# A diffusion trunk step with routed experts: column halves of each weight slot in the rounds of 64 expert slots, and a fourth column group of the large rounds that starts one step later

## What is computed

```
def moe_ffn(h, router, w_gu, w_down):
    logits = (h @ router).astype(jnp.float32)
    top_v, top_i = lax.top_k(logits, TOP_K)
    w = jax.nn.softmax(top_v, axis=-1)
    combine = jnp.sum(jax.nn.one_hot(top_i, N_EXPERTS, dtype=jnp.float32) * w[..., None], axis=-2)
    gu = jnp.einsum('btd,edf->btef', h, w_gu)
    g, u = jnp.split(gu, 2, axis=-1)
    act = jax.nn.silu(g) * u * combine[..., None].astype(h.dtype)
    return jnp.einsum('btef,efd->btd', act, w_down)
```

## Time and profile before

| | |
|---|---|
| median of 3 runs | 2507.28 us (2504.83 to 2510.34) |
| the profiled execution: its time, its span | 2505.68 us, 2503.8 us |
| TensorE (PE) busy | 2269.1 us, 91% of the span |
| PE's share of the chain that ended last | 85% |
| DMA moved | 552.11 MB, mean 221 GB/s |
| rounds 0 to 6 on PE, with the start of the wide round, in the two expert layers | 811.86 us to about 1156, 2071.54 us to about 2415 |

### The profile page before, as it was taken

The page is one execution under the profiler, slowest core; times in us unless marked ns, Lnnn a source line. Parts: engine busy times, 40 slices in busy tenths (PEclk is TensorE's granted clock), DMA queues, the critical chain, the costliest instruction groups (busy, mean ns, idle before and its releaser), DMA issues.

```text
span 2503.8 us, 44069 instructions
## 1 busy us (share of the span) xinstructions
PE 2269.1 (91%) x19591; PEld 1626.1 (65%) x19591; DVE 473.9 (19%) x1344; ACT 394.2 (16%) x829; POOL 67.2 (3%) x111
## 2 busy tenths in 40 slices
PE   5998998999998998899799589999988989989897
PEld 3875667888887544445475478888868875434354
DVE  1323432000113200000202320002334432000001
ACT  1122223000101000000202320001133320000000
POOL 5000000000000000000100000000000000000000
PEclk8999999999998999999899589999999989999998
DMA  9759787653354899997677176513430067999981
GB/s 321 217 197 391 281 314 202 199 151 101 113 194 139 291 380 338 385 331 275 184 237 292 37 209 194 151 34 118 151 101 7 11 219 254 384 337 381 334 322 42
DMA packets 356158, 552.11 MB, mean 221 GB/s; under 512 B 11392, under 2 KB 311168, under 8 KB 343472
## 3 DMA queue, kind: packets, MB, share of 16 engines
q1 hardware_dynamic: 344208, 525.31, 60.7%
q0 software_dynamic: 5840, 18.11, 2.8%
q10 hardware_dynamic: 5920, 5.78, 0.7%
HBM read 537.64 MB, written 15.98 MB: 221 GB/s over the span
## 4 chain that ended last, share of the span: by engine, by line
PE 85%; DVE 5%; DMA 3%; ACT 3%; issue 3%; ACTq 0%; POOL 0%; SPq 0%; DVEq 0%; POOLq 0%
PE ps L632 83%; DMA ring<-in_ada_w 2%; ACT ring L1362 2%; ACT work L1362 1%; PE ps L1002 0%; DVE ring L1908 0%; DMA work<-y_rows,work 0%; DVE work L1771 0%; DMA y_rows<-work 0%; DVE ring L1913 0%; DVE ring L1898 0%; DVE ring L2043 0%; ACT hT L1362 0%; PE ps L1099 0%; DVE ring L1890 0%
## 5 line engine op out<-in xcount | busy, mean ns | idle before, releaser
L632 PE MATMUL ps<-ring,work 128*32 128x384 f32 (+6 forms) x7752 | 710.4, 453 | 69.1 <-issue 37.4
L632 PE MATMUL ps<-hT,ring 128*128 128x256 f32 x3200 | 704.9, 380 | 3.2 <-ACT hT L1362 2.1
L632 PEld LDWEIGHTS ps<-hT,ring 128*128 128x128 f32 x3200 | 607.0, 190 | 98.2 <-ACT work L1362 6.9
L632 PEld LDWEIGHTS ps<-ring,work 128*32 128x32 f32 (+2 forms) x7752 | 339.6, 116 | 415.0 <-issue 292.0
L1362 ACT ACTIVATE work<-ps 128x256 f32<-128x256 f32 (+5 forms) x252 | 108.7, 444 | 1433.5 <-PE ps L632 1266.9
L632 PE MATMUL ps<-work,ring 128*128 128x256 f32 (+1 forms) x1344 | 290.9, 376 | 10.8 <-DVE work L1975 6.2
L632 PEld LDWEIGHTS ps<-work,ring 128*128 128x128 f32 (+1 forms) x1344 | 243.9, 189 | 48.3 <-DVE work L1975 8.6
L632 PE MATMUL ps<-ring 64*64 64x64 f32 (+1 forms) x4192 | 185.3, 230 | 17.6 <-ACT ring L1362 7.2
L632 PEld LDWEIGHTS ps<-ring 64*64 64x64 f32 x4192 | 162.6, 139 | 57.0 <-ACT ring L1362 24.2
L1362 ACT ACTIVATE ring<-ps 128x512 f32<-128x512 f32 (+3 forms) x224 | 106.9, 483 | 351.7 <-PE ps L632 315.3
L632 PE MATMUL ps<-ring,csil 128*2 128x512 f32 x768 | 98.2, 601 | 22.7 <-DMA ring<-in_ada_w 22.7
(11 more groups left out here) (253 smaller groups left out, 966.6 us busy)
## 6 DMA issues: line engine op xcount, KB each, us to landing
ring<-in_moe_w_gu SPq DMA_DIRECT2D x96, 1536.0 KB, 13.7
ring<-in_ada_w SPq DMA_DIRECT2D x96, 1024.0 KB, 7.6
ring<-in_moe_w_down SPq DMA_DIRECT2D x48, 1536.0 KB, 16.0
ring<-in_ff_w_gu SPq DMA_DIRECT2D x88, 512.0 KB, 5.8
ring<-in_dn_w_in SPq DMA_DIRECT2D x32, 1024.0 KB, 5.5
ring<-in_moe_w_gu SPq DMA_DIRECT2D x32, 1024.0 KB, 8.5
ring<-in_ff_w_down SPq DMA_DIRECT2D x44, 512.0 KB, 6.8
ring<-in_moe_w_down SPq DMA_DIRECT2D x32, 512.0 KB, 10.1
```

The lines of the kernel that those rows point to most:

```text
L632: return pe.matmul(out, lhsT, rhs, start=start, stop=stop, **kw)
```

## The change

- `columns` and `gate_up` (large): step 0 leaves the fourth column group idle. In steps 1 and 2 that group does two matmuls, 256 and 128 columns wide (`D_PARTS`), so that its 3 x 256 columns are done in two steps. The wait for slots 2 and 3 moves to step 1. Of silu, product, transposes and copy, steps 1 and 2 cover all 128 partitions; silu and the product are now one operation each instead of two. `down(3)` finds the last two blocks of its input by `D_AT`.
- Small rounds go through the same three steps as the large ones. `halves` gives two column groups one half of a slot and the other two groups the other half: 192 columns for a slot of 384, and in step 1 also 128 for a `_D` slot. `p_gu` counts up after each slot, and after each of the two `_D` slots in step 1.
- There are three turns in a small round instead of two, and each is built of pieces of 64 rows (`turn_small`), with four or five copies on ScalarE (`turned_small`) where there was one.
- SP no longer waits for `p_dn` before it loads slots 2 and 3.

The core of the diff:

```
                         for j in (0, 1, 4, 5, 2, 3, 6, 7, 8, 9, 10):
                             if j in GU_FREE:
                                 sp.wait_ge(moe["p_gu"], (done[0] + r) * 6 + GU_FREE[j])
-                                if j in (GATE_D, UP_D):
-                                    sp.wait_ge(moe["p_dn"], (done[0] + r) * 4 + 1)
...
                 def columns(q, s, j, j_d, bank):
                     landed(q, j)
-                    if s == 0:
+                    if s == 1:
                         landed(q, j_d)
...
                     for k in range(KC):
                         for b in range(STEPS):
-                            mm(ps[BLK * b:BLK * (b + 1), bank, 0:GW], xg[:, k, BLK * b:BLK * (b + 1)], w[:, k, :],
-                               k == 0, k == KC - 1)
-                        ins = mm(ps[CAP:P, bank, 0:DW], xg[:, k, BLK * s:BLK * (s + 1)], w_d[:, k, :],
-                                 k == 0, k == KC - 1)
+                            ins = mm(ps[BLK * b:BLK * (b + 1), bank, 0:GW], xg[:, k, BLK * b:BLK * (b + 1)], w[:, k, :],
+                                     k == 0, k == KC - 1)
+                        for n, (b, at, c, width) in enumerate(D_PARTS.get(s, ())):
+                            ins = mm(ps[CAP:P, bank, at:at + width], xg[:, k, BLK * b:BLK * (b + 1)],
+                                     w_d[:, k, c:c + width], k == 0 and n == 0, k == KC - 1, skip_group_check=True)
...
+                def halves(q, j, width, bank, at):
+                    landed(q, j)
+                    w = weights(j, 2 * width)
                     for k in range(KC):
+                        for x in range(2):
                             for b in range(2):
                                 t = 2 * x + b
+                                ins = mm(ps[BLK * t:BLK * (t + 1), bank, at:at + width], xg[:, k, BLK * b:BLK * (b + 1)],
+                                         w[:, k, x * width:(x + 1) * width], k == 0 and at == 0, k == KC - 1,
+                                         skip_group_check=True)
+                    return ins
...
+                    for j, j_d, bank in ((GATE[s], GATE_D, PG[s]), (UP[s], UP_D, PU[s])):
+                        ins = halves(q, j, HW, bank, 0)
+                        if s == 1:
+                            ins = halves(q, j_d, P, bank, HW)
+                        ins.then_inc(moe["p_gu"], 1)
...
                 def turn_small(q, s):
+                    pe.wait_ge(moe["d_act"], q * 3 + (s + 1))
...
+                    lo, hi = slice(0, 64), slice(64, P)
+                    pe.transpose(ps[:, 6, 0:P], ma_s[:, s, 0:P], ident)
                     if s == 1:
+                        pe.transpose(ps[:, 6, HW:HW + P], ma_s[:, s, HW:HW + P], ident)
+                    pe.transpose(ps[lo, 6, 64:P], ma_s[lo, s, P:HW], ident[lo, lo])
+                    pe.transpose(ps[:, 7, 0:64], ma_s[hi, s, 64:HW], ident[hi, hi])
+                    ins = mm(ps[hi, 7, 64:P], ma_s[hi, s, 0:64], ident[hi, hi])
+                    ins.then_inc(moe["p_tr"], 1)
...
                 def small(q):
...
+                    gate_up_small(q, 0)
+                    gate_up_small(q, 1)
                     turn_small(q, 0)
                     down_small(q, 0)
+                    gate_up_small(q, 2)
+                    turn_small(q, 1)
+                    down_small(q, 1)
                     pe.wait_ge(moe["d_g"], q + (i + 2))
                     gather(0)
                     gather(1)
+                    turn_small(q, 2)
+                    down_small(q, 2)
+                    down_small(q, 3)
...
+                def turned_small(q, s):
+                    act.wait_ge(moe["p_tr"], q * 3 + (s + 1))
+                    act.wait_ge(moe["p_dn"], q * 4)
+                    lo, hi = slice(0, 64), slice(64, P)
+                    f(ma_T[:, s, 0:64], ps[:, 6, 0:64], ACT.Copy)
+                    f(ma_T[lo, s, 64:P], ps[lo, 6, 64:P], ACT.Copy)
+                    if s == 1:
+                        f(ma_T[:, s, HW:HW + P], ps[:, 6, HW:HW + P], ACT.Copy)
+                    f(ma_T[:, s, P:HW], ps[:, 7, 0:64], ACT.Copy)
+                    f(ma_T[hi, s, 64:P], ps[hi, 7, 64:P], ACT.Copy).then_inc(moe["a_at"], 1)
```

More of the change, by code:

```diff
@@ L1097, in turn @@
                         pe.wait_ge(moe["a_at"], q * 3 + s)
-                    for c in range(2):
-                        pe.transpose(ps[:, 6, c * P:(c + 1) * P], ma_s[:, s, c * P:(c + 1) * P], ident)
-                    pe.transpose(ps[:, 6, 2 * P:2 * P + CAP], ma_s[0:CAP, s, 2 * P:3 * P], ident[0:CAP, 0:CAP]) \
-                        .then_inc(moe["p_tr"], 1)
+                    rows = P if s else CAP
+                    for c in range(3):
+                        ins = pe.transpose(ps[:, 6, c * P:c * P + rows], ma_s[0:rows, s, c * P:(c + 1) * P],
+                                           ident[0:rows, 0:rows])
+                    ins.then_inc(moe["p_tr"], 1)
                 def down(q, s, first):
@@ L1113, in down @@
                         for b in range(STEPS):
[L1114 to L1115 removed]
+                            of, at = (s, P * (c % 3) + BLK * b) if s < 3 else (D_AT[c, b][0], P * D_AT[c, b][1] + CAP)
+                            lhsT = ma_T[:, of, at:at + BLK]
                             for g in range(4):
@@ L1128, in columns_small @@
                                 t = 2 * x + b
-                                ins = mm(ps[BLK * t:BLK * (t + 1), bank, 0:width], xg[:, k, BLK * b:BLK * (b + 1)],
-                                         weights(j, width)[:, k, :], k == 0, k == KC - 1)
-                    ins.then_inc(moe["p_gu"], done)
-                def turn_small(q, s):
-                    pe.wait_ge(moe["d_act"], q * 3 + (1 + 2 * s))
-                    if s == 1:
-                        pe.wait_ge(moe["a_at"], q * 3 + 1)
-                    for c in range(2 if s else 3):
-                        ins = pe.transpose(ps[:, 6, c * P:(c + 1) * P], ma_s[:, s, c * P:(c + 1) * P], ident)
-                    if s == 1:
-                        ins = pe.transpose(ps[:, 6, 2 * P:2 * P + 64], ma_s[0:64, s, 2 * P:3 * P], ident[0:64, 0:64])
-                    ins.then_inc(moe["p_tr"], 1 + s)
+                                ins = mm(ps[BLK * t:BLK * (t + 1), bank, at:at + width], xg[:, k, BLK * b:BLK * (b + 1)],
+                                         w[:, k, x * width:(x + 1) * width], k == 0 and at == 0, k == KC - 1,
+                                         skip_group_check=True)
@@ L1566, in gated @@
                         act.wait_ge(moe["d_act"], q * 3 + s)
-                    f(mg_s[0:CAP, DW:GW], ps[0:CAP, PG[s], DW:GW], ACT.Silu)
-                    f(mg_s[:, 0:DW], ps[:, PG[s], 0:DW], ACT.Silu).then_inc(moe["a_silu"], 1)
+                    rows = P if s else CAP
+                    f(mg_s[0:rows, :], ps[0:rows, PG[s], 0:GW], ACT.Silu).then_inc(moe["a_silu"], 1)
                 def turned(q, s, first):
@@ L1573, in turned @@
                         act.wait_ge(moe["p_dn"], q * 4)
-                    f(ma_T[:, s, 0:2 * P + CAP], ps[:, 6, 0:2 * P + CAP], ACT.Copy).then_inc(moe["a_at"], 1)
+                    if s == 0:
+                        f(ma_T[:, s, :].rearrange("p (c n) -> p c n", c=3)[:, :, 0:CAP], ps4(6)[:, 0:3, 0:CAP], ACT.Copy) \
+                            .then_inc(moe["a_at"], 1)
+                    else:
+                        f(ma_T[:, s, :], ps[:, 6, 0:GW], ACT.Copy).then_inc(moe["a_at"], 1)
                 def output(q):
@@ L1600, in store_small, with gated_small @@
                             .then_inc(moe["y_out"], 16)
+                def gated_small(q, s):
+                    act.wait_ge(moe["p_gu"], q * 6 + (2 * s + 1))
+                    act.wait_ge(moe["d_act"], q * 3 + s)
+                    f(mg_s[:, 0:SW[s]], ps[:, PG[s], 0:SW[s]], ACT.Silu).then_inc(moe["a_silu"], 1)
+                def turned_small(q, s):
[8 more added lines that the diff above has]
+                    f(ma_T[hi, s, 64:P], ps[hi, 7, 64:P], ACT.Copy).then_inc(moe["a_at"], 1)
                 def small(r):
@@ L1604, in small @@
                     output(q - 1)
[L1605 to L1607 removed]
+                    gated_small(q, 0)
                     store(q - 1, r - 1)
[L1609 to L1615 removed]
+                    gated_small(q, 1)
+                    turned_small(q, 0)
+                    gated_small(q, 2)
+                    turned_small(q, 1)
                     tokens(q + 1)
[L1617 to L1618 removed]
+                    turned_small(q, 2)
                 def body(r, first):
@@ L2224, in gated @@
                         dve.wait_ge(moe["p_tr"], q * 3 + (s - 2))
-                    tt(ma_s[0:CAP, s, DW:GW], mg_s[0:CAP, DW:GW], ps[0:CAP, PU[s], DW:GW], ALU.mult)
-                    tt(ma_s[:, s, 0:DW], mg_s[:, 0:DW], ps[:, PU[s], 0:DW], ALU.mult).then_inc(moe["d_act"], 1)
+                    rows = P if s else CAP
```

(6 more changed lines are left out.)

73 lines of the change are left out of this document (26 added, 47 removed).

## The result

| | before | after |
|---|---|---|
| median, 8 runs each | 2507.78 us (2504.78 to 2510.34) | 2518.69 us (2516.34 to 2526.11) |
| ratio, 95% interval | | 1.005 (1.0037 to 1.0064) |
| the profiled execution: time, span | 2505.68, 2503.8 us | 2518.7, 2516.9 us |

The change makes the kernel slower by 0.5%. I had said 2509, range 2496 to 2523, with 0.35 for slower. Of the ten executions of a later run (e8) one took 3050.63 us at a mean granted clock of 0.739 of full speed and is left out of that run's ratio.

What follows compares the result with a forecast made beforehand. TensorE (PE), busy 91% of the span, was taken as the bound, with instruction fetch stalling it at loop tops. Terms +7.8 + 0.8 + 2.4 - 8.2 = +2.8 us on 2505.68 gave 2508.5, stated as 2509, range 2496 to 2523.

Steps and rivals of the forecast that it cites:

- columns, turns, one join more: Small rounds: narrower columns save 1.5 us, three turns and one more join cost 2.8; +1.3 each, +7.8 us for six.
- large rounds: Large rounds: five matmuls stand where four did, 0.1 us a round, +0.8 us for eight.
- slots 2 and 3 due later, SP: Weight loads: slots 2 and 3 needed 10.3 us later and SP's wait dropped; 0, since PE waits for no weight.
- code blocks between jumps: Small rounds, steps 0 and 1: three instruction blocks used in 4.6 us each, fetched in 5.2; 0.4 each, +2.4 us.
- the four tops: Loop tops, two per layer: moved within their code blocks, shortening the second wait, 3.5 each layer 1, 0.6 layer 3; -8.2 us.
- rival 1: Small rounds: code cannot keep up at 6 us per block, each losing 2.6 us; +13, 2522 us, chance 0.22.
- Rival 2: Small-round turns: shape changes and copies at their upper bound; +12, 2520 us, chance 0.13.
- high bound: Small-round turns: 0.3 us for each shape change and no overlap of copies; +4.8 us a round instead of +2.8.
- Rival 3: Turns and loop tops: cheap turns, and a jump losing its second wait in both layers; 2497 us, chance 0.18.
- Rival 4: Loop tops: weights cost PE after all, releasing slots singly gives back up to 7 us each; 2480 us, chance 0.07.
- the last step: Final sum: profiled 2505.68 us plus 2.8 gives 2508.5; median before 1.6 above that execution; forecast stated as 2509.

Runs made afterwards that it cites:

- e8: The changed kernel with each small-round turn as three 128x128 transposes and one copy of 384 columns, as before the change: 2503.30 us, ratio 0.9986.
- e4: The changed kernel with TensorE's loop over rounds 1 to 6 written out, other engines keeping theirs: 2480.47 us, ratio 0.99.
- e7: The changed kernel loading only part of each weight slot from round 1 on, so DMA is lightly loaded: 2484.04 us, one execution.
- e11: The kernel before, loading only part of each weight slot from round 1 on, as in e7: 2484.82 us, one execution.
- e2: The kernel before with only the large rounds of the change, all small rounds as before: 2482.30 us, ratio 0.9913.
- e9: e2 (large rounds of the change, small rounds of before) with TensorE's loop written out: 2462.88 us, ratio 0.9834.
- e12: e9 with the large rounds' wait for slots 2 and 3 put back from step 1 to step 0: 2472.88 us, ratio 0.9866.
- e10: The changed kernel with small rounds leaving out the 64 matmuls of step 1 on slots 2 and 3: 2484.49 us, one execution.
- e1: The changed kernel with the large rounds of before, so only the small rounds are changed: 2521.25 us, ratio 1.0058.
- e5: The kernel before with 16 unused matmuls added at TensorE's start, which shift all later code: 2486.64 us, ratio 0.9922.
- e6: The changed kernel with the same 16 unused matmuls at TensorE's start as e5: 2510.06 us, ratio 1.0016.

## Why the prediction was right or wrong

In the rounds I forecast +2.8 us and 10.8 are measured. By its own steps, in the change itself and with TensorE's loop written out:

| step | forecast | measured in the change | with e4 for the code |
|---|---|---|---|
| columns, turns, one join more | +1.3 x 6 | +1.2 x 6 (e7 against e11) | the same |
| large rounds | +0.1 x 8 | +0.03 each (e2 against before), part of the 1.2 | the same |
| slots 2 and 3 due later, SP | 0 | 0; 10 us once there is no jump (e9, e12) | |
| code blocks between jumps | +0.4 x 6 = +2.4 | +11.4 | +2.7 x 6 = +15.9 |
| the four tops | -8.2 | -8.1 | -13.9 |

The third column is an estimate, worked out from the rounds of the change and the 39.32 us of e7. The first small rounds are 5.3 and 2.2 us above that. In the four rounds with a top I count as code the last gap before the turn (1.08, 0.81, 1.00 and 0.25 us) and the 0.36 us in each of the two of layer 3; the rest of what they are above 39.32 is the top. The fourth column takes the rounds of e4 less 39.32 as the code, and the rounds of the change less those of e4 as the tops; 1.2 us are left over in the first small rounds. The two differ since behind a top the gap is shorter than the gaps in the same round of e4 (1.39, 1.26, 2.43 and 1.74 us in all): a block has come while PE waited for the jump. By both, one step is off by far more than the others.

**The step that failed is "Code blocks, between jumps", and in it the time of one block.** I had the demand right (three blocks in 13.9 us, 4.6 each) and put 5.2 against it, the time of one block behind a jump. In the run of a small round it is 6.2 us, as in rival 1: the packets start that far apart, and so do the two gaps of the first small round. By my own sum that makes 3 x 1.6 = 4.7 us at worst instead of 1.7. The rest of the step stood up better. I let what is there ahead cover 1.3 us. Steps 0 and 1 take 15.7 to 17.0 us in the rounds of e4, against 14.0 counted alike in e7: they are 1.7 to 3.0 us late and not 4.7, so 1.7 to 3.0 were covered, and e10 shows the cover too. With 6.2 in place of 5.2 my sum would have said 3.4 us a round; 2.7 are measured in e4. And one thing I had left out altogether: behind a late block the clock can fall (2.9 us once in the change, 1.3 in e4). The Trainium skill, Runtime: NRT & Kernel Launch, section Instruction fetch mechanics, gives PE a buffer of 128 KiB, which is eight blocks of 16 KiB; if they were filled ahead, e4 would show no gaps, and it shows at least one in each small round. The runs disagree with that reading.

**The tops.** My rule (how many instructions are left) had the right sign in both layers and was confirmed by moving them, in e1, e2, e5 and e6. In the change itself its size was right too: by the third column 3.7 and 4.6 us came back in layer 1 (forecast 3.5 each), and +0.2 and -0.4 in layer 3 (forecast 0.6 each). In layer 3 the 26 MATMULs cover 2.8 us and the second wait fell from 3.7 to 2.65, but little of that is left in the time.

**Rivals.** Rival 1 happened: it said 2522, with 2.6 us per round. Without jumps 2.7 are measured; in the change it is 5.3 and 2.2 us in the first small rounds and 0.6 to 1.4 behind a top, 11.4 in all and not 15.6, which takes 4 us off the 2522. Rival 2 did not: the turns cost 1.63, 1.81 and 1.49 us, 2.55 more per round, near the 2.7 taken. What the Trainium skill, TensorEngine Tiling (Array Packing), section Tiling Modes, says of the drain at a change of mode would have moved the turns toward the high bound; the rows stay with 1.6 us. Rival 3's cheap jump came in layer 1 alone. Rival 4 is refuted for this kernel, since weights wait for PE and not PE for weights, and is what one meets as soon as the jumps are gone.

The chance of 0.22 for rival 1 was too low: a row already said 5.2 > 4.6, and no row of the profile before had the time of a block in the run of a round, so 5.2 was not a figure to lean on. That the time is in the range is no credit to the sum: it is there because the range had been drawn to take in rival 1. One slip in the last step besides: 2508.5 and the 1.6 us by which the median before lay above the profiled execution make 2510, not 2509.

## What to carry to other kernels

Splitting matmuls for the sake of width has a price that no busy time shows: count the code blocks that a stretch runs through, and compare the time per block with what the trace shows while DMA is full (here blocks used in 5.2 us were in time and blocks used in 4.6 us were not). Before a change near a loop is judged, move the loop's top by some useless instructions, or write the loop out: here that alone was worth 20 and 34 us, more than anything the change computes. A wait that costs nothing now may be the next bound: try the change again once the present bound is gone.

## What the runs showed of the hardware

- The jump at the top costs 11.6 to 12.5 us in the kernel before: 5.4 to 5.5 of it until the first block, 3.6 to 3.7 until the second, and the rest at half clock. Over all kernels with full DMA the first wait is 5.0 to 5.5 us and the second 0 to 4.5, by where the top lies (e1, e2, e5). With DMA lightly loaded the first wait is 3.0 to 3.8 us and the second 1.1 to 1.4.
- While DMA moves some 370 to 400 GB/s, packets of code start 6.1 to 6.8 us apart in steps 0 and 1 (the change, e10), each with 1.0 to 1.1 us in its queue; where the rest of the 6 us goes, no row shows. PE waits when it uses a block in 4.6 us, and does not when it uses one in 5.2.
- Behind such a wait of 1.4 to 2.0 us the clock fell to half in single rounds (10.88 us for a row of 7.98 in the change, 9.68 in e1, e6 and e8, 9.31 in e4), and behind as long a wait it stayed up in others (7.98 in e6, e8 and e4), with the long turn as with the short one. Where it strikes stays open.
